# Half of a layer norm's scaling moved from ScalarE to VectorE, and one batch of transposes moved between two column halves

## The reference

```python
def layer_norm(x, g, b):
    xf = x.astype(f32)
    mu = xf.mean(-1, keepdims=True)
    var = jnp.square(xf - mu).mean(-1, keepdims=True)
    return ((xf - mu) * lax.rsqrt(var + LN_EPS) * g + b).astype(x.dtype)

def swiglu(h, w_in, w_out):
    g, u = jnp.split(h @ w_in, 2, axis=-1)
    return (jax.nn.silu(g) * u) @ w_out
```

## Time and profile before

| | |
|---|---|
| time, median of 3 runs | 1247.75 us (1244.14 to 1251.18) |
| the profiled execution: its time | 1245.37 us |
| the profiled execution: its span | 1243.7 us, mean granted TensorE clock 0.993 |
| TensorE busy | 1200.2 us, 96% of the span |
| VectorE busy | 675.1 us, 54% |
| ScalarE busy | 503.0 us, 40% |
| GpSimd busy | 53.8 us, 4% |

### The profile page before, as it was taken

How to read it: one execution, slowest core, us unless ns; L and a number is a source line. 1 busy time by engine, 2 the same in 40 slices (tenths; PEclk the granted TensorE clock), 3 DMA queues, 4 the chain that set the end, 5 groups by cost and what they waited for, 6 DMA issues and landing times.

```text
span 1243.7 us, 16572 instructions
## 1 busy us (share of the span) xinstructions
PE 1200.2 (96%) x6586; PEld 827.0 (66%) x6586; DVE 675.1 (54%) x1222; ACT 503.0 (40%) x763; POOL 53.8 (4%) x103
## 2 busy tenths in 40 slices
PE   6999899999999999999999999999999999999997
PEld 2697688887789877888878787445544444454446
DVE  5689968887679786764566675211211111111126
ACT  1478654444555575344347384111111111111125
POOL 0100101000000000001001200000000000000000
PEclk9999999999999999999999999999999999999998
DMA  9997868988646455765557779999999999999990
GB/s 368 388 338 275 311 222 307 346 311 324 246 171 249 173 219 184 280 219 204 198 201 269 250 304 397 410 426 426 424 425 425 427 411 425 427 424 426 425 412 35
DMA packets 50987, 394.98 MB, mean 318 GB/s; under 512 B 6673, under 2 KB 8913, under 8 KB 11378
## 3 DMA queue, kind: packets, MB, share of 16 engines
q1 hardware_dynamic: 39618, 337.18, 67.7%
q0 software_dynamic: 9072, 53.92, 12.1%
q10 hardware_dynamic: 2240, 3.10, 1.0%
HBM read 390.68 MB, written 3.49 MB: 317 GB/s over the span
## 4 chain that ended last, share of the span: by engine, by line
PE 84%; DVE 8%; ACT 3%; DMA 3%; issue 1%; SPq 1%; ACTq 0%; DVEq 0%
PE psum L1357 18%; PE psum L770 10%; PE psum L773 10%; PE psum L777 10%; PE psum L1403 9%; PE psum L1289 5%; PE psum L1297 2%; PE psum L825 2%; PE psum L829 2%; PE psum L827 2%; DMA staged<-in_ada 2%; DVE w_parts L2113 2%; DVE aring L2096 1%; PE psum L1056 1%; PE psum L1068 1%; PE psum L1047 1%
## 5 line engine op out<-in xcount | busy, mean ns | idle before, releaser
L2113 DVE TENSOR_TENSOR w_parts<-w_raw,w_parts 128x2048 fp32r<-128x2048 f32 x106 | 241.7, 2287 | 73.1 <-ACT w_parts L1493 73.1
L1493 ACT ACTIVATE w_parts<-w_raw 128x2048 fp32r<-128x2048 f32 x106 | 202.0, 1911 | 80.5 <-DMA w_raw<-in_units 80.5
L1357 PE MATMUL psum<-slabs,arena 128*64 128x512 f32 x768 | 222.5, 592 | 0.0
L770 PE MATMUL psum<-w_parts,h_parts 128*128 128x512 f32 x416 | 165.7, 398 | 2.4 <-ACT h_parts L1493 1.3
L773 PE MATMUL psum<-w_parts,h_parts 128*128 128x512 f32 x416 | 163.2, 392 | 0.0
L1357 PEld LDWEIGHTS psum<-slabs,arena 128*64 128x64 f32 x768 | 71.8, 137 | 109.2 <-issue 109.1
L1493 ACT ACTIVATE arena<-psum 128x512 f32<-128x512 f32 (+1 forms) x43 | 23.8, 557 | 245.4 <-PE psum L1376 140.0
L777 PE MATMUL psum<-w_parts,h_parts 128*128 128x512 f32 x416 | 111.8, 391 | 0.7 <-DVE h_parts L2290 0.7
L2096 DVE CUSTOM_DVE_ANT_0 aring<-aring,cb 128x1024 f32<-128x1024 f32 x80 | 94.5, 1219 | 2.0 <-DMA aring<-in_ada 1.9
L770 PEld LDWEIGHTS psum<-w_parts,h_parts 128*128 128x128 f32 x416 | 78.6, 189 | 20.3 <-DVE w_parts L2113 2.1
L777 PEld LDWEIGHTS psum<-w_parts,h_parts 128*128 128x128 f32 x416 | 78.1, 188 | 17.8 <-DVE h_parts L2290 1.3
(11 more groups left out here) (333 smaller groups left out, 1878.0 us busy)
## 6 DMA issues: line engine op xcount, KB each, us to landing
w_raw<-in_units SPq DMA_DIRECT2D x110, 1024.0 KB, 5.2
slabs<-in_w SPq DMA_DIRECT2D x52, 1024.0 KB, 14.4
slabs<-in_w SPq DMA_DIRECT2D x22, 2048.0 KB, 20.0
aring<-in_ada POOLq DMA_DIRECT2D x40, 1024.0 KB, 5.6
arena<-in_w SPq DMA_DIRECT2D x16, 2048.0 KB, 18.8
w_odd<-in_w SPq DMA_DIRECT2D x16, 2048.0 KB, 19.2
w_odd<-in_w SPq DMA_DIRECT2D x24, 1024.0 KB, 24.1
staged<-in_ada SPq DMA_DIRECT2D x8, 1024.0 KB, 18.6
```

Source lines behind the costliest of these rows:

```text
L770: mm(psum[:, bank, :], high(tile, tok), w_hi(k)[:, col:col + 512], start=first and bank not in begun, stop=False, skip_group_check=True)
L1357: ins = nc.tensor.matmul(psum[s * CAP:(s + 1) * CAP, w, :], xe_t[:, kt, s * CAP:(s + 1) * CAP], up_weights(w, s, b, kt), start=kt == 0, st ...
L1493: return nc.scalar.activation(out_ap, in_ap, func, **kw)
L2113: v.tensor_tensor(w_lo(k), raw(k), w_hi(k).bitcast(F32), ALU.subtract).then_inc(w_split, 1)
```

## The change

In norms 0, 1 and 2, ScalarE normalises only the second half of the columns. VectorE normalises the first half, with one `tensor_scalar` (multiply, then add, both with a scalar for each partition) at the end of `ln_scale`, behind a wait for its own shift. TensorE's transposes of the first half wait for a semaphore of VectorE's, `normed_first`, those of the second half for ScalarE's. `new_x` waits for both. Norm 3 is made by other functions and is not touched. Apart from that, in the first layer the transposes of norm 1, tile 0, move from ahead of `from_act(0, 10, 1)` to between its two column halves.

```diff
@@ normed_tiles, TensorE @@
                 for c in range(2):
-                    pe.wait_ge(normed, 4 * q + 2 * t + c + 1)
+                    if c:
+                        pe.wait_ge(normed, 4 * q + 2 * t + 2)
+                    else:
+                        pe.wait_ge(normed_first, normed_first_from + 2 * q + t + 1)
@@ from_act, TensorE @@
                 for cs in ((0,), (1,)) if last else ((0, 1),):
+                    if layer == 0 and t == 1 and cs == (1,):
+                        normed_tiles(1, 0)
                     ins = to_tokens(k, [(s, 1024 * s + 512 * c, 2 * t + c) for s in range(2) for c in cs], t,
@@ order behind the feed-forward, TensorE @@
                 from_act(layer, 9, 1)
-                if layer == 0:
-                    normed_tiles(1, 0)
                 from_act(layer, 10, 1)
@@ ln_normed, ScalarE @@
                 act.wait_ge(ln_shift, 2 * q + t + 1)
-                for c in range(2):
-                    r = resid[:, t, c * 512:(c + 1) * 512]
-                    A(r, r, Id, scale=moments[:, t, 3:4], bias=moments[:, t, 4:5]).then_inc(normed, 1)
+                r = resid[:, t, 512:1024]
+                A(r, r, Id, scale=moments[:, t, 3:4], bias=moments[:, t, 4:5]).then_inc(normed, 2)
@@ ln_scale, VectorE @@
                 stt(moments[:, t, 4:5], moments[:, t, 0:1], -1.0, moments[:, t, 3:4], ALU.mult, ALU.mult).then_inc(ln_shift, 1)
+                dve.wait_ge(ln_shift, 2 * q + t + 1)
+                v.tensor_scalar(resid[:, t, 0:512], resid[:, t, 0:512], moments[:, t, 3:4], moments[:, t, 4:5], ALU.mult,
+                                ALU.add).then_inc(normed_first, 1)
@@ new_x, VectorE @@
+                dve.wait_ge(normed_first, normed_first_from + 2 * q + t + 1)
                 dve.wait_ge(normed, 4 * q + 2 * t + 2)
```

More of the change, by code:

```diff
@@ L371, in build @@
         forget_split, forget_split_from = staged_in[4], 16
+        normed_first, normed_first_from = staged_in[3], 32
         head_rooted, head_rooted_from = staged_in[0], 32
```

## The result

| | before | changed |
|---|---|---|
| time, median of 21 runs each | 1244.69 us (1243.37 to 1251.18) | 1250.44 us (1247.53 to 1256.23) |
| ratio to before, 95% interval | | 1.0042 (1.0033 to 1.0052): 5.2 us longer |
| the profiled execution: time, span, clock | 1245.37, 1243.7, 0.993 | 1248.97, 1247.2, 0.993 |

The change makes the kernel 0.4% slower: less than the 0.5% within which the prediction called the result the same, but the ratio's interval is clear of 1. The ratio is the measure from here on, since each series of runs has its own executions of the kernel before beside it. The 1247.75 us of before were a median of 3 runs, 1244.69 us is one of 21.

A forecast was written before the change was run, and what follows sets the result against it. The prediction took VectorE's chain, whose split releases TensorE around the norms, as the bound. Delays of +1.9 us and one more clock fall of 1.7 gave +3.6 us on 1247.75, hence 1251.3 us, range 1245.5 to 1255.5.

The forecast's parts named there:

- What bounds: Around the norms: VectorE's chain has no gap in norm 0, and TensorE's weight load waits for VectorE's split in all three.
- The price of one half, 0.53 us: Each new VectorE instruction, 486 ns long and starting 0.20 us behind the shift, makes VectorE 0.53 us late.
- Norm 0, +1.06: Norm 0: VectorE's two halves delay the split behind tile 1's shift, and TensorE with it, by 1.06 us.
- Norm 1, -0.23: Norm 1: tile 1's sums start 0.76 us sooner, its half costs 0.53, so TensorE's load for unit 51 comes 0.23 us sooner.
- the column half "made early": Norm 1: VectorE's 0.30 us wait for TensorE behind the high part goes, as TensorE makes the needed column half early.
- Norm 2, +1.06: Norm 2: tile 0's transposes come 0.6 us sooner, but VectorE's chain delays the split at tile 1 by 1.06 us.
- The sum of the delays, +1.9: All three norms together: +1.06 - 0.23 + 1.06 = +1.9 us.
- One fall more, +1.7: Waits ahead of a split in the three norms: one more costly fall of TensorE's clock than before, 1.7 us.
- TensorE's earlier transposes reach the end: Rival: the splits do not bind, so the norms gain 4.7 us, 8.1 without falls; 1239.7 to 1243.0 us; chance 0.09.
- the change does nothing: Rival: the weight stream absorbs the delays later; within 0.3 us of 1247.75; chance 0.04.
- The delay without another fall: Rival: +1.9 us, or +0.2 if norm 2's fall goes too; 1247.9 to 1249.7 us; chance 0.27.
- The third, that all three fall: Rival: clock falls in all three stretches and the new instruction takes 0.69 us; +6.4 us, 1254.1; chance 0.16.

The follow-up runs named there:

- twice: The changed kernel with a second such VectorE instruction, on a buffer nobody reads again, behind the new one in all six places; ratio to before 1.0065 (1.0050 to 1.0080).
- only_vector: The changed kernel without the move of norm 1's transposes, so VectorE's half alone against the kernel before; ratio to before 1.0046 (1.0028 to 1.0064).
- pool_timed: The kernel before, with GpSimd making tile 0's second low part in norms 0, 1 and 2, started behind VectorE's add; ratio 0.9970 (0.9957 to 0.9984).
- only_move: The kernel before with only the transposes of norm 1, tile 0, moved; ScalarE makes both halves; ratio to before 1.0007 (0.9996 to 1.0017).
- before_fill: The kernel before with six surplus TensorE matmuls ahead of tile 1's transposes in norms 0 and 2; ratio to before 0.9977 (0.9960 to 0.9994).
- tile0_only: The kernel before with VectorE making the first half only at tile 0 of norms 0 and 2, no transposes moved; ratio 1.0012 (0.9999 to 1.0024).
- tile1_only: The kernel before with VectorE making the first half only at tile 1 of norms 0 and 2, no transposes moved; ratio 1.0019 (1.0006 to 1.0033).

## Why the prediction was right, and where not

The result came out as predicted: slower, and by less than 0.5%. The forecast was 3.6 us more than before and 1251.3 us; measured were 5.2 us more by the ratio and 1250.44 us. That the times agree within 0.9 us is luck: the forecast stood on a median of before that was 3 us high, which hid a sum that was too small. Step by step:

- **What bounds.** Right: VectorE's list around each norm, not ScalarE's half. `twice`, only_vector and pool_timed show it from both sides, with more and less work.
- **The price of one half, 0.53 us.** Measured 0.58. The start behind the shift was right (0.20 us), the length was 546 ns and not 486. Two scalars and two operators together cost 0.06 us more than the nearest row and stay far from the 691 ns of the upper bound. What the Trainium skill ("VectorE: DVE Perf Modes", the perf-mode tier table) says about a `tensor_scalar` holds here in kind: it is well under the two-tensor length.
- **Norm 0, +1.06.** Right: +1.12 where the clock does not fall, against 2 x 0.58 = 1.16 by the measured price. Tile 0's earlier transposes ended in the wait for `drv`, 2.80 us instead of 1.57, and TensorE waited 1.54 us for the first of `h_parts` instead of 0.39.
- **Norm 1, -0.23.** The step that failed. Of its three terms, the price was right (+0.58) and the high part came 0.27 us sooner, not 0.38 (VectorE's low part, which waits for it, starts 8.87 us behind the first sum instead of 9.14), and it was VectorE's half and not the move that brought it: only_vector has the same 8.87 us without the move, and only_move has 9.14. The third, 0.30 us of VectorE's wait for the column half "made early" and the overlap of 0.08 behind it, was taken for a gain of the move. It was part of the fall in the execution of before: TensorE's slow matmuls made that half late, and before_fill, in the old order, goes from the low part to the next sum in 0.61 us instead of 0.99; tile0_only, in the old order with a fall there, waits again (0.20 us). -0.27 + 0.58 is +0.31, and +0.34 was measured. The sentence that norm 1's fall "cost nothing" falls with it: it cost 34.73 less 34.35, 0.38 us (0.30 in tile0_only).
- **Norm 2, +1.06.** Right: +1.17 without falls. That the two profiled executions differ by only 0.12 us is luck of the falls. In before it cost 1.61 us; in the changed one it began during the transposes, so that a part passed while TensorE waited for the split (0.26 us left of that wait), and it cost 34.29 less 33.73, 0.56:

```profile
473.08 1.94 PE L956 MATMUL psum<-cst,resid_tm 128*128 128x128 f32 x8 [2.41 <-DVE resid_tm L2290]
...
475.28 0.79 PE L771 MATMUL psum<-w_parts,h_parts 128*128 128x512 f32 x1 [0.26 <-DVE w_parts L2116]
```

- **The sum of the delays, +1.9.** Measured +2.6; norm 1 makes 0.57 us of the difference of 0.7.
- **One fall more, +1.7.** Right in kind and undersized: 2.6 us over the runs. In the profiled executions there was exactly one more, in norm 0, worth 1.35 us; norm 1's moved from the first tile, where it cost 0.38, to the second, where it cost 1.44. The sentence that a fall behind any of the three "now costs in full" holds for norms 0 and 1 in the main, and not for norm 2's 0.56. A fall costs between 0.3 and 1.6 us of its 1.7, by what waits beside it.
- **The rivals.** That TensorE's earlier transposes reach the end is out: tile0_only and only_move show where each ends. That the change does nothing is out by the ratio's interval. The delay without another fall gives half of what was measured: 2.6 us, where the ratio's interval begins at 4.1. The third, that all three fall, is what the profiled execution showed, but with 0.58 us and not 0.69 as the price.
- **What the profile was to show.** The `tensor_scalar` ends ahead of ScalarE's half (139.48 against 139.79, at 0.55 us); features of norm 0, tile 0, start 3.87 us behind the shift instead of 3.29; no idle ahead of norm 1's first transposes; new waits of 1.30 and 1.10 us at its second. The weight load in norm 0 waits 1.34 us where 1.2 were foreseen (1.11 us in the matmuls' own row), but in norm 2 the row of the matmuls has 0.26, by the fall above.

What stays open is why a given waiting stretch ends in a fall in one execution and not in another: only_vector lost 3.4 us in norm 0, twice a usual fall and in one piece, and nothing in norm 1; tile1_only fell once in norm 0 and not in norm 2, with the same wait of 1.34 us behind both. The runs show that the falls are gone with the waits filled, not what decides.

## What to carry to other kernels

Ask of an instruction that changes engines what stands behind it in its new list, not how busy that engine is: VectorE was busy for 54%, and still its list set the end of the waits that counted here. A term read from one execution that holds a fall of the clock is a term of the fall as well; compare the same stretch of an execution without one before calling it slack or gain. Where TensorE must wait in a kernel that fills it otherwise, the wait can be paid twice, once as idle time and once as slow matmuls behind it.

## What the runs showed of the hardware

- A VectorE `scalar_tensor_tensor` with two SBUF inputs of 512 float32 columns takes 0.69 us, and 1.35 or 1.78 us where GpSimd's subtraction of 1.30 us had started 0.49 or 0.06 us ahead of it. GpSimd's own length was 1.30 us with such a meeting and without one. A VectorE `tensor_tensor` with one input in PSUM kept its 0.68 us beside it.
- Around the norms TensorE's granted clock fell to 0.5 in 20 of 35 profiled passages without surplus matmuls in the waits, and in none of 7 with them. By the ratios the surplus matmuls were worth 2.9 us to the kernel before and 5.5 us to the changed one, each uncertain by some 2 us.
- One usual fall loses 1.7 us of clock and lengthened the norm's stretch by 0.3 to 1.6 us, by what waited beside it.
- A `tensor_scalar` of 512 float32 columns takes 546 ns with two operators and two scalars for each partition, 486 ns with one.
